# Six of the modulation chunks are gathered around and inside the scan of a two-layer diffusion trunk, not between the input projections

## The reference, cut to what matters

```
m = silu(cond) @ mod_w[layer] + mod_b[layer]      # 1024 -> 3072, for two conditions
shift, scale, gate = split(m, 3)
x = x + gate * rms_norm(mixer(rms_norm(x) * (1 + scale) + shift))
```

## Time and profile before

| | |
|---|---|
| median of three runs | 1039.18 us (1038.46 to 1039.75) |
| the profiled execution | 1039.04 us, of which 1037.2 us from its first to its last instruction |
| TensorE busy | 1000.9 us of the span |
| VectorE, ScalarE, GpSimd busy | 585.7, 300.9, 120.5 us |
| granted TensorE clock, mean | 0.987 |

### The profile page before, as it was taken

The page is one execution under the profiler, slowest core; times in us unless marked ns, Lnnn a source line. Parts: engine busy times, 40 slices in busy tenths (PEclk is TensorE's granted clock), DMA queues, the critical chain, the costliest instruction groups (busy, mean ns, idle before and its releaser), DMA issues.

```text
span 1037.2 us, 13356 instructions
## 1 busy us (share of the span) xinstructions
PE 1000.9 (97%) x5201; PEld 724.3 (70%) x5201; DVE 585.7 (56%) x1245; ACT 300.9 (29%) x774; POOL 120.5 (12%) x170
## 2 busy tenths in 40 slices
PE   8999999999999999999999999999999989999997
PEld 3445666454665576887988888788999646566786
DVE  3755655898965579677388233431767436453113
ACT  3153110201113345531301134113310567354111
POOL 4010000030300152100052111200000200010001
PEclk8999999999999999799999999999999999999999
DMA  9662455120222200100052203720501100000102
GB/s 277 225 189 69 142 183 163 40 63 20 82 92 82 81 1 1 41 2 21 9 176 78 107 1 122 226 71 1 162 21 63 55 1 0 1 1 1 41 1 102
DMA packets 68423, 78.11 MB, mean 75 GB/s; under 512 B 2700, under 2 KB 64135, under 8 KB 68360
## 3 DMA queue, kind: packets, MB, share of 16 engines
q1 hardware_dynamic: 63810, 68.96, 21.0%
q0 software_dynamic: 2432, 7.56, 2.2%
q10 hardware_dynamic: 2117, 0.73, 0.3%
HBM read 73.74 MB, written 3.51 MB: 74 GB/s over the span
## 4 chain that ended last, share of the span: by engine, by line
PE 86%; DVE 8%; ACT 4%; issue 1%; DMA 1%; ACTq 0%; POOLq 0%; DVEq 0%; POOL 0%
PE ps L1362 77%; PE ps L1555 4%; PE ps L1392 2%; PE ps L2001 1%; DVE xreg L2589 1%; DMA phase<-in_hyena_sin_freq 1%; DVE phase L2597 1%; ACT phase L1325 1%; ACT hT L949 1%; PE ps L1402 1%; DVE xreg L2249 1%; DVE pad L2514 1%; DVE pad L2521 0%; DVE xreg L2613 0%; DVE phase L2850 0%
## 5 line engine op out<-in xcount | busy, mean ns | idle before, releaser
L1362 PE MATMUL ps<-hT,wring 128*128 128x128 f32 (+4 forms) x1072 | 264.4, 405 | 2.5 <-ACT hT L949 2.5
L1362 PEld LDWEIGHTS ps<-hT,wring 128*128 128x128 f32 x1072 | 159.8, 192 | 101.2 <-issue 93.3
L1362 PE MATMUL ps<-phase 128*128 128x512 f32 (+4 forms) x760 | 209.3, 423 | 13.7 <-ACT phase L877 2.5
L1362 PEld LDWEIGHTS ps<-phase 128*128 128x128 f32 (+1 forms) x760 | 129.0, 192 | 82.0 <-issue 52.2
L1362 PE MATMUL ps<-wring,mix 128*128 128x256 f32 x560 | 122.1, 379 | 0.8 <-DVE mix L2858 0.8
L1362 PEld LDWEIGHTS ps<-wring,mix 128*128 128x128 f32 x560 | 106.0, 190 | 15.7 <-DVE mix L2858 1.6
L1362 PE MATMUL ps<-phase,hT 128*128 128x256 f32 (+3 forms) x336 | 78.9, 391 | 2.4 <-DVE hT L2225 1.7
L1362 PEld LDWEIGHTS ps<-phase,hT 128*128 128x128 f32 x336 | 60.5, 190 | 18.4 <-issue 13.3
L1362 PE MATMUL ps<-hT,phase 128*128 128x64 f32 (+4 forms) x276 | 55.8, 345 | 0.0
L1555 PE MATMUL ps<-ident,phase 128*128 128x128 f32 x400 | 51.1, 280 | 2.0 <-ACT phase L1328 1.1
L1555 PEld LDWEIGHTS ps<-ident,phase 128*128 128x128 f32 x400 | 46.5, 145 | 9.0 <-issue 4.8
(11 more groups left out here) (385 smaller groups left out, 1316.7 us busy)
## 6 DMA issues: line engine op xcount, KB each, us to landing
wring<-in_mod_w SPq DMA_DIRECT2D x24, 1024.0 KB, 5.2
wring<-in_even_in_w SPq DMA_DIRECT2D x16, 1024.0 KB, 7.5
wring<-in_odd_in_w SPq DMA_DIRECT2D x5, 1024.0 KB, 9.3
phase<-in_odd_in_w SPq DMA_DIRECT2D x4, 1024.0 KB, 7.3
wring<-in_odd_out_w SPq DMA_DIRECT2D x4, 1024.0 KB, 5.2
wring<-in_even_out_w SPq DMA_DIRECT2D x3, 1024.0 KB, 9.4
xreg<-in_x_sample SPq DMA_DIRECT2D x1, 2048.0 KB, 15.0
xreg<-in_x_sample POOLq DMA_DIRECT2D x1, 2048.0 KB, 11.1
```

What stands on the lines that cost most here:

```text
L1362: return nc.tensor.matmul(o, l, r, start=first, stop=last)
```

## The change

`LATE` keeps (1,0), (1,1) and (0,8) to (0,11), in `hv0`, `hv1` and `hx10`. The six chunks (1,2) to (1,7) become `SCANNED`. No chunk is left in `hx11`, `hx20` and `in_q1`. SCANNED[0] is gathered in front of the second solve group, where `keep_busy` does two products and not three; SCANNED[1] behind the solve, in front of the scan; SCANNED[2] to [5] in steps 1 to 4 of the scan, between Uinv r and kd v. They are not turned by transposes and summed on VectorE: `pick_modulation` multiplies the copied rows, as the stationary operand, with `pick`, a 128 x 2 table of zeros and ones, so that TensorE sums the quarters, and ScalarE adds the bias while it reads the bank (`take_scanned`). `pick` is made once on VectorE from the identity. The loads of SCANNED go through one slot in the region `phase`, and the loads of the output projection `even_out_w` stand behind them in SP's list. `scale_factors(1)` moves behind the scan, `gate_factors(0)` to where it was.

```diff
-LATE = [(1, j) for j in range(8)] + [(0, j) for j in range(8, 12)]
+LATE = [(1, j) for j in range(2)] + [(0, j) for j in range(8, 12)]
+SCANNED = [(1, j) for j in range(2, 8)]
...
+def scan_steps():
+
+    fills = [("scan0.a", 2), ("scan0.b", 4)]
+    for i in range(1, NT):
+        fills += [("scan%d.a" % i, 6), col(SCANNED[i]), row(SCANNED[i + 1]), ("scan%d.b" % i, 4 if i < NT - 1 else 2)]
+    return fills
...
+        rows_at.update({which: pflat[:, 1024:1024 + WC] for which in SCANNED})
...
+            lst += [modulation_chunk(which) for which in SCANNED[0:5]]
             for j in range(4):
+                if j == 3:
+                    lst.append(modulation_chunk(SCANNED[5]))
                 lst.append((a["even_out_w"][0], WC * j, WC, out_f[0][4 * (NT - 1) + j]))
...
-        slot_of += range(WSLOTS + 1)
+        slot_of += [WSLOTS] * 5 + [0, 1, 2, WSLOTS, WSLOTS]
...
+                if last == row_f[SCANNED[0]]:
+                    wait_full(sp, inv_groups[0]["levels"][-1] + CHAINS[0] - 1)
...
+            def take_scanned(which):
+
+                layer, j = which
+                f = col_f[which]
+                wait_full(act, f)
+                for m in range(2):
+                    ins = nc.scalar.activation(modc_l[layer][:, 2 * j + m, :], bank(f)[:, 2 * m:2 * m + 2], ACT.Identity,
+                                               bias=vec1[:, 24 * layer + 2 * j + m:24 * layer + 2 * j + m + 1])
+                ins.then_inc(free(f), 1)
...
-            for n in range(3):
+            for i in range(1, NT):
+                take_scanned(SCANNED[i])
+                take_modulation_rows(SCANNED[i + 1])
+                if i == 1:
+                    square_heads(0)
+            for n in (1, 2):
                 square_heads(n)
+            take_scanned(SCANNED[-1])
...
+            def pick_modulation(which):
+
+                f = col_f[which]
+                wait_free(pe, f)
+                pe.wait_ge(pick_ready, 1)
+                wait_drained(pe, row_f[which])
+                for m in range(2):
+                    ins = mm(bank(f)[:, 2 * m:2 * m + 2], rows_at[which][:, m * P:m * P + P], pick[:, :])
+                ins.then_inc(full(f), 1)
...
-                keep_busy(g["T1"], 3 if g is inv_groups[1] else 1)
+                keep_busy(g["T1"], 2 if g is inv_groups[1] else 1)
...
-
+                    gather_modulation(SCANNED[0])
+
+            pick_modulation(SCANNED[0])
+            gather_modulation(SCANNED[1])
             wait_drained(pe, last_U[-1])
...
+                if i:
+                    pick_modulation(SCANNED[i])
+                    gather_modulation(SCANNED[i + 1])
                 for d in range(2 if i < NT - 1 else 0):
                     wait_drained(pe, fs[4 + d])
...
+            pick_modulation(SCANNED[-1])
             turn_heads(0)
...
+            for which in SCANNED:
+                wait_drained(dve, col_f[which])
+            scale_factors(1)
             dve.wait_ge(xback_in, 32)
```

More of the change, by code:

```diff
@@ L85 @@
     + [("hT0", 2 * NT)] + with_two("hv0", 0) + [("ab", 2)] + with_two("hv1", 2, 7) + [("tr_ab", 2)] + with_two("hx10", 4, 7) + [("tr_hv", NT)] \
-    + with_two("hx11", 6, 7) + with_two("hx20", 8, 7) \
+    + [("hx11", 7), ("hx20", 7)] \
     + [("tr_hx", NT), ("fft0", 10), ("hx21", 3), ("hg0", 3), ("fft0_back", 5), ("fft1", 10), ("hg1", 3),
-       ("in_q0", 3), ("fft1_back", 5)] + with_two("in_q1", 10) + [
-         ("in_k0", 3), ("cumsum", 1), ("tr_q", NT), ("in_k1", 3), ("in_v0", 3), ("tr_k", NT),
+       ("in_q0", 3), ("fft1_back", 5), ("in_q1", 3), ("in_k0", 3), ("cumsum", 1), ("tr_q", NT), ("in_k1", 3), ("in_v0", 3), ("tr_k", NT),
          ("sums01", 4), ("keys01", 4), ("in_v1", 3), ("sums23", 4), ("in_z1", 3), ("sums4", 2),
@@ L122, in scan_fill @@
 def scan_fill(start, step, k):
-    skipped = 4 if step == 0 else 2 if step == NT - 1 and k >= 8 else 0
-    return start["scan"] + 10 * step - (4 if step else 0) + k - skipped
+    if k < 6:
+        return start["scan%d.a" % step] + k - (4 if step == 0 else 0)
+    return start["scan%d.b" % step] + k - (8 if step == NT - 1 else 6)
 def unit_fills(start):
@@ L258, in program @@
         eps = sb("eps", [P, 3])
+        pick = sb("pick", [P, 2])
         phase = sb("phase", [P, 28704])
@@ L473, in program @@
         spec_f = [[start["spec%d" % (5 * o + j // 2)] + j % 2 for j in range(10)] for o in range(2)]
-        row_f = {which: start[row(which)[0]] for which in EARLY + LATE + LAST}
-        col_f = {which: start[col(which)[0]] for which in EARLY + LATE + LAST}
+        row_f = {which: start[row(which)[0]] for which in EARLY + LATE + SCANNED + LAST}
+        col_f = {which: start[col(which)[0]] for which in EARLY + LATE + SCANNED + LAST}
         turned_f = [start["hT0"] + n for n in range(2 * NT)], \
@@ L562, in chunk_list @@
             for n in range(5):
-                lst += [late.pop(0), (even, columns[n + 1], WC, hy_last[n + 1]), late.pop(0)]
+                lst += late[2 * n:2 * n + 1] + [(even, columns[n + 1], WC, hy_last[n + 1])] + late[2 * n + 1:2 * n + 2]
             for half, f in enumerate(hy_gates):
@@ L883, in take_modulation_rows @@
                         wait_full(act, col_f[group[group.index(which) - 2]])
+                if which in SCANNED[1:]:
+                    wait_full(act, col_f[SCANNED[SCANNED.index(which) - 1]])
                 f = row_f[which]
@@ L999, in _ @@
                     copy_even_first(n)
-                    take_modulation_rows(LATE[2 * n])
-                    take_modulation_rows(LATE[2 * n + 1])
+                    for which in LATE[2 * n:2 * n + 2]:
+                        take_modulation_rows(which)
                 else:
@@ L1110, in _ @@
                     take_gates(start["in_z0"], 0)
+                    take_modulation_rows(SCANNED[0])
+            take_scanned(SCANNED[0])
+            take_modulation_rows(SCANNED[1])
             def square_heads(n):
@@ L2164, in _ @@
             take_modulation((0, 0))
+            dve.wait_ge(ident_in, 16)
+            nc.vector.tensor_reduce(pick[:, :], ident[:, :].rearrange("p (q c) -> p c q", q=4)[:, 0:2, :], AXX, ALU.add)\
+                .then_inc(pick_ready, 1)
             def scale_factors(layer):
@@ L2328, in _ @@
                         sum_even_chunk(n + 1)
[L2329 removed]
+                    if 2 * n < len(LATE):
+                        take_modulation(LATE[2 * n])
                     add_even_last(n)
```

45 lines of the change are left out of this document (22 added, 23 removed).

## The result

The kernel with the change takes 1029.90 us (median of three, 1028.34 to 1030.32), before 1039.18 us. The ratio is 0.9907, with a 95% interval of 0.9885 to 0.993. The forecast was 1031.8 us. The profiled execution of after took 1030.32 us, of which 1028.5 us are span; it is 8.72 us under that of before.

What follows compares the result with a forecast made beforehand. TensorE bounds the kernel: dense projections shorten by what is removed, the scan's holes take added work free. Terms -5.73 - 3.77 + 0 + 0 + 1.7 + 0.45 = -7.35 us gave 1031.8 us, range 1029.3 to 1035.6 us.

Steps and rivals of the forecast that it cites:

- `hx11` and `hx20`: Dense projections: removing four gathers and four turns shortens the kernel by 5.73 us.
- a gather is 1.00 us: Projections hx11 and hx20: each gather removed was priced at 1.00 us, each turn in the stream at 0.22 us.
- `in_q1`: Projection in_q1: removing two gathers, two turns and a wait for ScalarE's row copy saves 3.77 us.
- the rival in which VectorE paces `in_q1`: VectorE's convolution holds the next projection up, so the 3.77 us stay: 1035.5 us, or about 1038 us; chance 0.08.
- the pick's bounds: A pick costs between 0.22 and 0.82 us, which puts the kernel's time between 1030.8 and 1034.2 us.
- In front of the second group and of the scan: New work there hides in TensorE's waits of 0.96 us (0.87 us left) and 1.54 us; cost 0.
- The scan's steps: Steps 1 to 4: pick and gather, 1.45 us each step, fill 4.1 us of holes; 1.7 us are lost.
- The pick: Scan: two products of two columns take 0.45 us; the one behind the scan adds 0.45 us to the path.
- The loads: Scan chunks share one slot; with one step's lead over the even_out_w loads, the sixth chunk causes no wait.
- The rival's price of 3.2 us: Scan: the sixth chunk lands up to 3.2 us late behind three even_out_w loads, time 1035.0 us; chance 0.10.
- the missing fall: First solve group: the clock no longer falls, saving about 5.0 us, time 1026.8 us; chance 0.10.
- The price of a fall in the second group: Second solve group: the clock falls there, costing 9.9 us, time 1041.7 us; chance 0.06.

Runs made afterwards that it cites:

- the filling of four: Kernel after, with four unused 512-column products in the first solve group's hole, where TensorE waits for ScalarE; 1024.76 us, ratio to before 0.9868.
- e14_both_holes_filled: Kernel after, with unused products cut to fit both holes of the first solve group's first level; 1025.01 us, ratio to before 0.9864.
- three products: Kernel after, with three unused products in the hole of the first solve group; 1029.42 us, ratio to before 0.9907.
- e1_hx_gathers_twice: Kernel before, with each of the four gathers in hx11 and hx20 issued twice in a row; 1042.84 us, ratio to before 1.0037.
- e7_before_filled_two: Kernel before, with two unused 512-column products in the hole of the first solve group; 1038.16 us, ratio to before 0.9999.

## Why the prediction was right, point by point

**`hx11` and `hx20`: right, 0.58 us too small.** The step "a gather is 1.00 us" took the distance from the gather's start to the next start, which leaves out what its neighbours lose: 0.09 us ahead and 0.10 us behind. Three full pairs of edges and the one ahead of the last gather are about 0.7 us; the last pair had been put 0.1 us too high (2.07 for 1.97 us by the timeline).

**`in_q1`: right, 0.42 us too small,** for the same reason, two gathers with 0.2 us of edges each. No wait took the place of the one removed, so the rival in which VectorE paces `in_q1` is refuted. These two terms put the time 0.9 us under the 1030.8 us that the pick's bounds allowed at the least. The range took it in at the end that had been left open for a shorter fall of the clock; the profiled fall was not shorter, so in that the range held partly by luck.

**In front of the second group and of the scan: right.** The idle time in the lead went from 0.96 to 0.60 us, for 0.87 us in the forecast, and the start moved with all the rest. The 1.54 us in front of the scan were filled without a loss: from the solve's last products to the scan's first it is 508.04 - 504.88 = 3.16 us with the new work and 507.47 - 504.32 = 3.15 us without. It was close, and in part luck: with the doubled pick, 0.44 us longer there, the same way took 507.60 - 504.06 = 3.54 us, so less than 0.1 us of room had been left.

**The scan's steps: mechanism right, +1.00 us for +1.7 us.** The step said 9.20 + 1.45 = 10.65 us; it is 10.47 us. A record of 80 products is 9.20 us long, but when another product follows without a wait, that one starts 9.04 us after it: 519.12 - 510.08. The last 0.16 us of a record lie beside the next. So each hole was 0.16 us larger than the idle time shown, 4.1 + 4 x 0.16 = 4.7 us, and 4 x 1.43 - 4.7 = 1.0 us. That the rest is lost one for one, the doubled gathers showed. Step 4 has no kd v; there pick and gather stand in front of intra v and, behind the hole, straight on the way to the gates.

**The pick: right,** 0.43 us in a step and 0.40 us behind the scan, for 0.45 us. The upper end of what its bounds give is 1034.0 us by the forecast's own terms (0.28, 3.2 and 0.82 us), not 1034.2 us; nothing else rests on it.

**The loads: right that the sixth chunk comes in time,** and that the lead is why. The rival's price of 3.2 us was too low: without the lead 5.3 us, as the issues ahead of it cost 2.2 us more, and a fall of the clock.

**The clock: right that it falls in the first group and not in the second.** The price of the missing fall, 5.0 us, was also met, with 5.1 us by the filling of four, 4.9 us by that of both holes and 5.3 us by the traces of these, but by luck in its parts. It let the 64 products alone gain 12.14 - 7.18 us. In e14_both_holes_filled they and the second hole take 419.85 - 411.20 = 8.65 us, in after 423.10 - 411.21 = 11.89 us, so 3.2 us come from there; 2.0 us more come from the transposes and products behind them, which the forecast had left out. The argument against it was not complete either: "the wait before it is untouched" holds, but there are two holes, and a fall followed either, so closing the one alone would not have kept the clock up. The price of a fall in the second group, 9.9 us, was wrong. It let the clock stay down through a whole level and the transposes, 18.0 us and more; 2.53 us of idle time brought a fall of 3.5 us, which cost 1.2 us.

## What to carry to other kernels

Price a step by the difference of two stretches with and without it, not by its own record or the distance to the next start: a gather among dense products takes 0.19 us from its neighbours, and a record overlaps the next. Where an engine's wait is filled, look for the wait of the next engine behind it; here filling both was worth 5 us, and filling the first alone nothing clear of the spread. A load into a shared slot needs its lead counted from the issue in front of it on the queue, not from the moment at which the slot is free.

## What was not expected of the hardware

The clock fell behind as little as 0.79 us of idle time (three products), and did not fall behind 0.96 us in front of the second group before. What tells these apart, the runs don't show. The same code brought falls of different length: 13.6 us in the profile of after, 6.8 us in that of the kernel with doubled gathers in the scan, whose code is the same up to there. Ahead of everything that the change moves, at about 85 us, TensorE waits 2.5 us for ScalarE. Eleven of thirteen traces have a fall behind this wait, and two, those of e1_hx_gathers_twice and e7_before_filled_two, have none: there the way from this wait's end to `hx11` is 63.2 us, in before and after 64.9 us. With no change to the code, the time of before ran from 1036.88 to 1039.90 us over eight runs beside the first experiments; a fall that comes or stays away is worth about half of that. The Trainium skill (TensorE: Matmul & The Clock Gate, Part 1) says that activity is judged in windows that run free of the kernel's start. The runs agree in that position and length of the fall vary between executions of the same code; they do not show why a hole of 0.79 us is enough.

Going from 128-column to 32-column weights and back cost TensorE 0.32 us, of which only 0.13 us lie between the gather's start and the next start.
